# A second weight panel loaded behind the fourth x tile, and the first projection panel's products placed between the turns of x

## What is computed

```
h    = rmsnorm(x, norm_mix)                 # x * 1/sqrt(mean(x^2)+eps) * norm_mix
proj = h @ w_in                             # columns: q,k,v (1536), a,b (8), z, and the short convolution's
qkv  = silu(causal_dwconv(concat(state, proj[q,k,v]), w_conv_qkv))     # width 4
log_a, beta = from proj[a], proj[b]
... gated delta rule over q,k,v; gated norm with z; short convolution mixer
x = x + concat(o, y_sc) @ w_out             # then the MLP (4096 wide), a gate, a last norm
```

## Time and profile before

| | |
|---|---|
| time of three runs | 1432.56, 1432.43, 1430.95 us; median 1432.43 |
| profiled execution | 1430.81 us, of which the span shown in the profile is 1429.1 |
| TensorE busy | 1408.0 us, 99% of the span |
| VectorE, ScalarE, GpSimd busy | 713.5, 486.0, 181.4 us |
| chain that ended last | PE 93%, DVE 2%, ACT 1%, issue 1% |

### The profile page before, as it was taken

One profiled execution on the slowest core, in us unless ns is written; L12 is line 12 of the kernel. 1 busy time (PEld: TensorE's weight loads), 2 busy tenths in 40 slices (PEclk: granted clock), 3 DMA queues, 4 the chain that ended last, 5 costly groups with the idle time before them and its releaser, 6 DMA issues.

```text
span 1429.1 us, 25603 instructions
## 1 busy us (share of the span) xinstructions
PE 1408.0 (99%) x9822; PEld 1386.8 (97%) x9822; DVE 713.5 (50%) x1319; ACT 486.0 (34%) x890; POOL 181.4 (13%) x249
## 2 busy tenths in 40 slices
PE   7999999999999999999999999999999999999998
PEld 7999999999999999999999999999999999999997
DVE  5678846866846436333333333333333333347454
ACT  6324355344244226331230311303213022136445
POOL 3200211224233321000000000000000000041220
PEclk9999999999999999999999999999999999999999
DMA  7112314321223541211111111111111111211113
GB/s 187 47 43 60 104 50 135 84 82 40 81 94 74 115 95 30 60 44 44 45 44 44 44 58 46 45 44 45 44 44 45 53 46 49 74 46 40 36 30 122
DMA packets 166335, 89.90 MB, mean 63 GB/s; under 512 B 50779, under 2 KB 160283, under 8 KB 166246
## 3 DMA queue, kind: packets, MB, share of 16 engines
q1 hardware_dynamic: 165238, 84.89, 21.5%
q0 software_dynamic: 1008, 3.79, 0.7%
HBM read 77.97 MB, written 10.69 MB: 62 GB/s over the span
## 4 chain that ended last, share of the span: by engine, by line
PE 93%; DVE 2%; ACT 1%; issue 1%; DVEq 0%; ACTq 0%
PE pg L767 68%; PE pg L886 16%; PE pg L1126 1%; DVE cv L1775 1%; PE bk L1031 1%; DVE act_lo L2136 1%; PE bk L936 1%; PE bk L1026 1%; PE bk L1013 1%; PE bk L1022 0%; PE bk L903 0%; PE bk L992 0%; PE bk L930 0%; PE bk L943 0%; PE bk L973 0%
## 5 line engine op out<-in xcount | busy, mean ns | idle before, releaser
L767 PE MATMUL pg<-act_hi,w_hi 128*128 128x352 f32 x1236 | 399.8, 323 | 5.0 <-DVE w_lo L1695 1.9
L767 PE MATMUL pg<-act_lo,w_hi 128*128 128x352 f32 x1236 | 396.2, 321 | 0.0
L767 PE MATMUL pg<-act_hi,w_lo 128*128 128x352 f32 x1212 | 388.2, 320 | 0.0
L767 PE MATMUL pg<-u_hi,w_hi 128*128 128x352 f32 x768 | 247.8, 323 | 0.0
L767 PE MATMUL pg<-u_lo,w_hi 128*128 128x352 f32 x768 | 246.4, 321 | 0.0
L767 PE MATMUL pg<-u_hi,w_lo 128*128 128x352 f32 x768 | 246.1, 321 | 0.0
L767 PEld LDWEIGHTS pg<-act_hi,w_hi 128*128 128x128 f32 x1236 | 231.9, 188 | 6.9 <-DVE w_lo L1695 2.2
L1271 ACT ACTIVATE w_hi<-w_raw 128x1024 fp32r<-128x1024 f32 x111 | 117.2, 1056 | 348.8 <-PE pg L767 314.5
L767 PEld LDWEIGHTS pg<-act_lo,w_hi 128*128 128x128 f32 x1236 | 232.3, 188 | 0.0
L767 PEld LDWEIGHTS pg<-act_hi,w_lo 128*128 128x128 f32 x1212 | 227.1, 187 | 0.0
L2209 DVE TENSOR_TENSOR xres<-xres,pg 128x352 f32 (+1 forms) x192 | 99.1, 520 | 196.1 <-PE pg L767 195.9
(11 more groups left out here) (372 smaller groups left out, 1661.9 us busy)
## 6 DMA issues: line engine op xcount, KB each, us to landing
w_raw<-in_w_up SPq DMA_DIRECT2D x32, 512.0 KB, 3.8
w_raw<-in_w_down SPq DMA_DIRECT2D x32, 512.0 KB, 3.3
w_raw<-in_w_in SPq DMA_DIRECT2D x29, 512.0 KB, 3.9
x_tok<-in_x_prompt SPq DMA_DIRECT2D x8, 512.0 KB, 7.0
w_raw<-in_w_out SPq DMA_DIRECT2D x8, 512.0 KB, 4.2
x_col<-in_x_prompt SPq DMA_DIRECT2D x32, 128.0 KB, 2.4
w_raw<-in_w_ple_gate SPq DMA_DIRECT2D x8, 512.0 KB, 4.0
out<-y_tok SPq DMA_DIRECT2D x5, 512.0 KB, 3.1
```

Source lines behind the costliest of these rows:

```text
L767: last = mm(pg[bank][:, 0:TH], w, a, start=i == 0, stop=i == len(terms) - 1)
```

## The change

SP issues the transfer of panel 1 behind that of x tile 3, ahead of tiles 4 to 8 (before: behind all of x and the two small states). ScalarE splits panel 1 after tile 3 (before: tile 5), VectorE after tile 4 (before: tile 6). TensorE makes `first_group(0)` in three pieces of 8 products, one behind the turns of each of the tiles 5, 6 and 7; `ab_group(1)` moves behind the turns of tile 8; `first_group(1)` moves ahead of `ab_group(2)`, and `first_group(2)` ahead of the norm's products. All three a and b groups now use bank `pg[2]`, so each waits until the one before has been copied out, and `first_group(2)` waits for the third. VectorE takes the thirds of panel 1 out of PSUM by plain copies (`first_third`), and when `r_b` is there it multiplies the whole by it in SBUF (`first_norm`). GpSimd's `keep_state` of panel 1 waits for that. The diff, blank lines and some unchanged ones left out:

```diff
@@ -474,7 +474,7 @@
-        CHAIN_ABS, CHAIN_LOG_A, CHAIN_BETA, CHAIN_G = 3, 20, 22, 24
+        CHAIN_ABS, CHAIN_LOG_A, CHAIN_BETA, CHAIN_G = 5, 22, 24, 26
         PARAMS = 16 * (6 + CW + SW)
@@ -614,9 +614,10 @@
                     load_w(0, 0, win_v[:, :, OFF_A:OFF_A + P], KD)
+                if t == 3:
+                    load_in(U_QKV)
             sp.dma_start(st_in[:, :], st_qkv[0].rearrange("b w f -> (b w) f")).then_inc(sm.states_in, 16)
             sp.dma_start(sc_in[:, :], st_sc[0].rearrange("b w f -> (b w) f")).then_inc(sm.states_in, 16)
-            load_in(U_QKV)
@@ -787,13 +788,20 @@
+                if n > 0:
+                    pe.wait_ge(sm.ab_kept, n)
                 terms = [(w_hi[0][:, k, :], a[:, k, cols(n)]) for k in range(KD) for a in (act_hi, act_lo)]
-                products(n, terms).then_inc(sm.ab_mm, 1)
-            def first_group(n):
-                pe.wait_ge(sm.ab_kept, n + 1)
-                products(n, parts(1, KD, 0, act_hi, act_lo, n)).then_inc(sm.mm_done, 16 if n == 0 else 4)
+                products(2, terms).then_inc(sm.ab_mm, 1)
+            def first_group(n, a=0, e=3 * KD):
+                if n == 2:
+                    pe.wait_ge(sm.ab_kept, 3)
+                for i, (w, m) in enumerate(parts(1, KD, 0, act_hi, act_lo, n)):
+                    if a <= i < e:
+                        last = mm(pg[n][:, 0:TH], w, m, start=i == 0, stop=i == 3 * KD - 1)
+                if e == 3 * KD:
+                    last.then_inc(sm.mm_done, 16 if n == 0 else 4)
@@ -825,12 +833,17 @@
-                if t in (4, 7):
-                    whole = 3 if t == 4 else 6
-                    pe.wait_ge(sm.xlo_even, whole)
-                    pe.wait_ge(sm.xlo_odd, whole)
+                if t == 4:
+                    pe.wait_ge(sm.xlo_even, 3)
+                    pe.wait_ge(sm.xlo_odd, 3)
                     panel_ready(0, 0)
-                    ab_group((t - 4) // 3)
+                    ab_group(0)
+                elif t in (5, 6, 7):
+                    panel_ready(U_QKV, 0)
+                    first_group(0, (t - 5) * KD, (t - 4) * KD)
+            pe.wait_ge(sm.xlo_even, 6)
+            pe.wait_ge(sm.xlo_odd, 6)
+            ab_group(1)
             pe.wait_ge(sm.states_in, 32)
@@ -838,12 +851,11 @@
             last.then_inc(sm.st_turned, 1)
-            panel_ready(U_QKV, 0)
-            first_group(0)
+            first_group(1)
             pe.wait_ge(sm.xlo_even, NTT + 1)
             pe.wait_ge(sm.xlo_odd, NTT + 1)
             ab_group(2)
-            first_group(1)
+            first_group(2)
             pe.wait_ge(sm.r_chain, 5)
@@ -854,7 +866,6 @@
             last.then_inc(sm.ab_turned, 1)
-            first_group(2)
             def row_turn():
@@ -1303,8 +1314,8 @@
                         .then_inc(sm.xhi_made, 1)
-                if t in (1, 5):
-                    split_w((t - 1) // 4, 0)
+                if t in (1, 3):
+                    split_w((t - 1) // 2, 0)
                 if 2 <= t < 6:
@@ -1715,7 +1726,7 @@
                     dve.wait_ge(sm.x_squared, 2)
-                nc.vector.tensor_copy(qkv[0:AB, 0, cols(n)], pg[n][0:AB, 0:TH]).then_inc(sm.ab_kept, 1)
+                nc.vector.tensor_copy(qkv[0:AB, 0, cols(n)], pg[2][0:AB, 0:TH]).then_inc(sm.ab_kept, 1)
@@ -1731,8 +1742,8 @@
                    act_hi[:, 0:4, t * P:t * P + n].bitcast(f32), SUB).then_inc(sm.xlo_even, 1)
-                if t in (2, 6):
-                    split_w((t - 2) // 4, 0)
+                if t in (2, 4):
+                    split_w((t - 2) // 2, 0)
                 if t in (5, 8):
@@ -1755,12 +1766,31 @@
+            def first_third(n):
+                a, e = n * TH, min(n * TH + TH, TP)
+                product_ready(U_QKV, 0, 4 * n + 4)
+                last = nc.vector.tensor_copy(pre[0][:, PAD + a:PAD + e], pg[n][:, 0:e - a])
+                if n == 2:
+                    last = nc.vector.tensor_copy(samples(pre[0])[:, :, PAD:SEG],
+                                                 pg[n][:, e - a:TH].rearrange("p (b t) -> p b t", t=NT))
+                last.then_inc(sm.evacuated, 16 if n == 0 else 4)
+            def first_norm():
+                dve.wait_ge(sm.r_chain, 9)
+                dve.wait_ge(sm.evacuated, 12 * U_QKV + 12)
+                now = pre[0][:, PAD:PAD + TP]
+                link(tt(now, now, r_b[:, 0:TP], MUL))
+                now = samples(pre[0])[:, :, PAD:SEG]
+                link(tt(now, now, r_b[:, TP:T].rearrange("p (b t) -> p b t", t=NT), MUL))
             def qkv_third(b, n):
                 if n == 0:
                     dve.wait_ge(sm.state_put, b)
                 product_ready(b, 0, 4 * n + 4)
-                to_columns(pre[(b - 1) % 2], n).then_inc(sm.evacuated, 16 if b == U_QKV and n == 0 else 4)
+                to_columns(pre[(b - 1) % 2], n).then_inc(sm.evacuated, 4)
@@ -1839,11 +1869,15 @@
-            dve.wait_ge(sm.r_chain, 9)
+            dve.wait_ge(sm.state_put, U_QKV)
+            for n in range(3):
+                first_third(n)
+            first_norm()
             dve.wait_ge(sm.params_in, PARAMS)
             for b in range(U_QKV, U_F):
-                for n in range(3):
-                    qkv_third(b, n)
+                if b > U_QKV:
+                    for n in range(3):
+                        qkv_third(b, n)
                 unit_done(b, 0)
@@ -2318,6 +2352,8 @@
+                if b == U_QKV:
+                    pool.wait_ge(sm.chain, 2)
                 x, j = (b - 1) % 2, feature(b)
```

## The result

| | median | lowest and highest | runs |
|---|---|---|---|
| before | 1431.86 us | 1430.77 to 1433.89 | 20 |
| changed | 1434.03 us | 1432.35 to 1438.13 | 20 |

A forecast was written before the change was run, and what follows sets the result against it. TensorE, busy 99%, bounds the kernel. Idle 2.9 us gone against 1.9 to 2.8 at the panel, 0.77 at the bank, 0.4 at tile 4: +0.25 on the median 1432.43 gives 1432.7 us; range 1430.8 to 1434.6.

The forecast's parts named there:

- rival (c): TensorE's clock falls to half pace behind the wait for panel 1: 1434.5 us, or 1437.1; chance 0.11.
- The forecast at 0.60: The main case, chance 0.60: 1432.7 us, with TensorE at full pace behind the wait for panel 1.
- The worse case of (c): Turns between panel 1's products delay the clock's return, costing 4.4 us: 1437.1 us; chance 0.05 of being over the bound.
- Steps 2 and 3: Panel 1's split on VectorE starts at 18.46, first product at 20.84; TensorE waits 1.9 to 2.8 us for it.
- (b): VectorE's split of panel 1 gets the port before GpSimd, takes 1.20 us, TensorE 1.12 us sooner: 1431.6 us; chance 0.14.
- step 2: Panel 1's w_lo on VectorE takes 2.32 us beside GpSimd's act_lo, so the panel is ready at 20.78.
- Step 4: TensorE's sequence from panel 1's first product at 20.84: pieces, turns and groups add up to 37.22 at ab_group(2)'s end.
- Step 1: Panel 1's earlier transfer makes x tile 4 come at about 13.6; TensorE gap of 0.3 to 0.5 us, hidden.
- Step 5: A new TensorE wait of 0.77 us ahead of first_group(2), for the copy out of the bank ab_group(2) filled.
- Step 6: The 1.45 us wait ahead of the norm's products is gone; panel 2 starts at 44.67, 0.25 us later.
- Step 7: VectorE's longer work ahead of panel 3, with first_norm, shrinks a cover of 1.06 us to 0.1; no wait counted.
- rival (d): VectorE's work ahead of panel 3 overruns, or each new switch on TensorE costs 0.1: up to 1 us, 1433.7; chance 0.11.

The follow-up runs named there:

- g1_again: The changed kernel again without an edit, run as the yardstick for variants on the same chip; 1433.78 us, ratio 1.0012 to the kernel before.
- e1_handover: The changed kernel with ab_group(2) moved ahead of first_group(1), so that the copy of the shared bank is covered; 1434.44 us, ratio 1.0016 to before.
- e3_split_first: The changed kernel with VectorE's w_lo of panel 1 moved ahead of tile 4's act_lo; 1431.83 us, ratio 0.9997 to before.
- g3_fill16: The changed kernel with 16 discarded products added ahead of TensorE's wait for panel 1; 1433.76 us, ratio 1.0008 to before.
- e2_transfer: The kernel before with only panel 1's transfer moved, issued behind x tile 3; 1431.65 us, ratio 0.9999 to before.
- the fills: The changed kernel with 12, 16 or 20 discarded products ahead of the wait for panel 1; 1434.06, 1433.76 and 1433.91 us.
- g2_handover2: The changed kernel with ab_group(2) ahead of first_group(1), the same edit as e1_handover, on another chip; 1432.99 us, ratio 1.0007 to before.
- g4_small_first: The changed kernel with only panel 0's small subtraction moved ahead of tile 2's act_lo on VectorE; 1433.89 us, ratio 1.0016 to before.
- e4_fill: The changed kernel with 12 discarded products of panel 0 added ahead of TensorE's wait for panel 1; 1434.06 us, ratio 1.0013 to before.

## Why the prediction came out in its range, and what it had wrong

The time lies in the range, 1430.8 to 1434.6, and within 0.2% of before, as it was given 0.92. But the predicted 1432.7 stood for +0.25 us, and +2.2 was measured. The range held because it took in the low end of rival (c), which had a chance of 0.11, and by some luck: it was laid around 1432.43, the median of three runs, 0.57 us above the 1431.86 of twenty. Laid around the latter, its top would be 1434.0, just where the time came out.

The prediction also named what would show it wrong, and the profiles show it: panel 2 was to start between 43.5 and 46.5 and starts at 48.10 (46.62 in g1_again, without the long subtraction), and products 0.3 us apart behind the wait were to be rival (c). So the time was right, and the way to it was not.

- **The failed step is the one that ranked rival (c).** The forecast at 0.60 took the wait to end at full pace, since 1.26, 1.45 and 1.87 us did. Rival (c) had the mechanism, the condition ("if the level falls there"), the price (1.8 us; it cost 1.4 to 1.6) and the time (1434.5; 1434.0 was measured), and was given 0.11. Its evidence was one execution. The 1.87 us wait of the earlier trace rows ended at full pace there by luck: in half of the profiles it doesn't. The three waits were counted as three proofs, and two of them were shorter. The worse case of (c), a slow return, is in none of the five profiles: full pace was back 3.0 to 3.5 us after the first slow product, turns between the products or not. But the three runs of the changed kernel at 0.995 took 1437.7 to 1438.1 us, where that case was priced at 1437.1. What happened in them stays open.
- **Steps 2 and 3.** Right. `w_lo` was predicted at 18.46 for 2.32 us; where the small subtraction took 0.22 it ran at 18.50 for 2.31 in e1_handover and at 18.54 for 2.30 in g1_again. The first product was predicted at 20.84 and went at 20.87 and 20.90. The wait, 1.9 to 2.8, was 1.86 to 2.40 in five profiles. (b), the split before GpSimd, happened in none: the neighbour was ahead whenever the text put the split behind `act_lo`. In e3_split_first the two don't meet, since the split ends at 18.55 and GpSimd starts at 19.12. One working of step 2 does not add up: 1.28 and 1.20 less the 0.04 between the starts are 2.44, not 2.32; the split ended 1.08 us behind GpSimd. The step went by the row's 2.32, so nothing hangs on it.
- **Step 4.** 44.67 for panel 2 is met to 0.2 us where the clock holds: g3_fill16 45.26 less 0.37 for tile 2 coming at 10.17 instead of 9.80 is 44.89.
- **Step 1** put tile 4 at 13.6 with a gap of 0.3 to 0.5; where tiles 2 and 3 were turned at the earlier pace it came at 13.9 to 14.6 with a gap of 0.30 to 0.46, and TensorE lost nothing by it. But the step had no term for tile 2. Tile 2 came at 9.80 and 9.82 in the two profiles with the old transfer order and at 9.89 to 10.57 in the twelve with the panel ahead of the later tiles. Why is open, and with two against twelve chance is not excluded. e2_transfer shows that the old order absorbs it; the new one, which waits for tile 4's split, passes it on.
- **Step 5.** Predicted 0.77 with the restart, measured 0.60 and a restart of 0.1. Right.
- **Step 6.** Right: no wait ahead of the norm's products.
- **Step 7, rival (d).** The sum came out at a cover of 0.1 us and no wait; the trace has a wait of about 0.3. `first_norm` and its two neighbours in the changed kernel, then TensorE at panel 3:

```profile
48.91 1.23 DVE L1784 TENSOR_TENSOR pre<-pre,r_b 128x1024 f32<-128x1024 f32 x1 [2.67 <-ACT r_b L1282]
50.17 0.19 DVE L1786 TENSOR_TENSOR pre<-pre,r_b 128x32 f32<-128x32 f32 x1
...
59.01 1.35 DVE L1763 TENSOR_TENSOR pre<-pg,r_b 128x352 f32<-128x352 f32 x3
```
```profile
59.50 0.32 PE L768 MATMUL pg<-act_hi,w_lo 128*128 128x352 f32 x1
59.68 0.40 PE L768 MATMUL pg<-act_hi,w_hi 128*128 128x352 f32 x1
59.92 0.33 PE L768 MATMUL pg<-act_lo,w_hi 128*128 128x352 f32 x1
```

  The 1.23 and 0.19 are the prediction's 1.20 and 0.18. The third of panel 2 that frees the bank is out at about 59.5, and TensorE's next product follows 0.18 us behind the last, the one after it 0.24 behind that: 0.1 us with the restart, and as much again in small pieces at the next panels' starts. From panel 2 on it is 1385.0 us against 1384.7. The "0.1 to 0.5 us if my sum is short" was it.

**The account.** Without a fall: 0.25 predicted, 0.37 for tile 2 (in g3_fill16; it varies), 0.22 of step 4, 0.25 behind panel 2, together 1.1 us; runs at 0.998 show 1.0. The fall adds 1.15 in the mean. That is 2.2, the difference of the medians. By the means of the 20 runs it is 2.5, and 2.0 without the three at 0.995, which this account leaves out. Of these the fall is shown by the fills, the panel wait by e3_split_first. The 0.22 of step 4 and the cause of tile 2's lateness were not tested.

**The small subtraction.** The Trainium skill, SBUF — State Buffer (section "SBUF: two separate sides"), says that whichever of GpSimd and a VectorE operation with two SBUF inputs starts first holds the shared pair of ports for the whole instruction. The rows agree on who is held up: 0.04 us behind GpSimd's start the small subtraction takes 1.31 us, 0.04 us ahead of it 0.22. They agree less well on for how long. Held until GpSimd's end at 14.94 and then 0.22 long, it would end at 15.16, and it ended at 15.02; and the other way round GpSimd took 1.32 us instead of 1.27, although 0.18 us of the subtraction were still to come. In the kernel before, 0.04 us between two starts kept the long case away.

## What to carry to other kernels

A wait of about 2 us in front of dense products costs more than its length here: price it with the fall behind it (1.5 us more, in most runs), and when one execution shows such a wait ending at full pace, count that as one draw and not as a rule. When a stage is moved earlier, look at where its last piece stands in the queue of the engine that makes it: the same order with `w_lo` one operation earlier on VectorE was 2.2 us faster, and with the bank wait covered too it beat the old one. Where runs fall on several levels, sort them by the granted clock before comparing medians.

## What the runs showed of the hardware

- The fall has no fixed place behind a wait. The first slow product is the one at 21.48 behind a first at 20.90 in g1_again, and the one at 21.93 behind 20.87 in e1_handover. In the changed kernel and g2_handover2 the first one itself is slow, 0.66 us where full pace has 0.43. In g4_small_first the granted clock, the third number from the end of the first row below, had fallen to 0.50 while TensorE still waited:

```profile
20.50:20.84 0.34, 0.00 (x0) 0.00 (x0) 0.34 (x2) 0.00 (x0) 0.00 (x0) 0.50 1.24 2
```
```profile
20.84 0.66 PE L802 MATMUL pg<-act_hi,w_hi 128*128 128x352 f32 x1 [2.40 <-DVE w_lo L1706]
```

  So first products at full pace behind a wait are no sign that the clock will hold.
- Five profiles of five had it in or behind the panel's wait of 1.86 to 2.40 us, 7 of 14 behind the late one of 1.86 to 1.88. Behind a wait of about 1.7 us for tile 4 it came once in two (the changed kernel, not e4_fill), behind e4_fill's 1.52 not. So the length of the last wait alone doesn't decide, and no border is drawn from this.
- The first rise of the clock is not fixed either. In the changed kernel and e4_fill tile 2's turns already ran at the later pace; in before they reached it 17 turns in the earlier trace rows. The column of the granted clock does not show this: it reads 1.00 over those turns at 0.21 us too, so ahead of the first rise only the pace tells.
- The same operation, `w_lo` of 128x1024, took 2.30 to 2.34 us behind `act_lo` in every kernel that had it there, with GpSimd's `act_lo` begun just ahead of it, and 1.22 with the order turned.
